# Front chunks of a hybrid trunk step: state inputs in two row groups copied out by ScalarE, scores and state outputs inside the first projection

## The reference

```python
proj = x @ w_in                                   # q, k, v (8 heads x 128) and u (1024)
attn = stick_breaking(q, k_all, v_all, q_pos, k_pos)
# per head: z = q k^T * scale; w = sigmoid(z) * prod of sigmoid(-z) of the later keys; out = w v
bu = einsum('blgc,gpc->blgp', u, b_bar)           # 64 groups x 64 complex states, 16 channels each
h = associative_scan(_linear_combine, (a, bu))    # h_t = lam_bar * h_(t-1) + bu_t
y = einsum('blgp,gcp->blgc', h, c).real + d_skip * u
z = gelu(y);  ssm = z * sigmoid(z @ w_glu + b_glu)
merged = [rms_norm(attn), rms_norm(ssm)]
```

## Time and profile before

| | us |
|---|---|
| median of 3 runs | 1701.26 |
| lowest, highest | 1698.42, 1701.41 |
| the profiled execution | 1701.27 |
| its span in the trace | 1699.5 |
| front: projection 0 of chunk 1 starts | 72.42 |
| front: last loop chunk ends | 383.58 |
| PE busy in the span | 1513.2 |

### The profile page before, as it was taken

How to read it: one execution, slowest core, us unless ns; L and a number is a source line. 1 busy time by engine, 2 the same in 40 slices (tenths; PEclk the granted TensorE clock), 3 DMA queues, 4 the chain that set the end, 5 groups by cost and what they waited for, 6 DMA issues and landing times.

```text
span 1699.5 us, 22977 instructions
## 1 busy us (share of the span) xinstructions
PE 1513.2 (89%) x8898; PEld 975.0 (57%) x8898; DVE 572.1 (34%) x1024; ACT 141.1 (8%) x296; POOL 225.8 (13%) x368
## 2 busy tenths in 40 slices
PE   8999999999999779999789898788898887889775
PEld 6777777777777546655445465454455454555333
DVE  7899988874210531111111021011112110111115
ACT  3111111113000300000000000000000000000001
POOL 4666666600000010000000000000000000000002
PEclk8999999999999889999999999999999999999997
DMA  7554544533496199999999999999999999999974
GB/s 182 152 139 110 147 120 118 139 98 102 143 303 221 40 346 412 404 416 415 416 400 416 418 404 410 415 414 405 399 417 411 389 417 413 412 407 412 417 271 171
DMA packets 175314, 520.04 MB, mean 306 GB/s; under 512 B 23504, under 2 KB 135248, under 8 KB 147952
## 3 DMA queue, kind: packets, MB, share of 16 engines
q1 hardware_dynamic: 160032, 485.73, 74.4%
q10 hardware_dynamic: 13056, 17.77, 3.3%
q0 software_dynamic: 2128, 15.21, 3.2%
HBM read 496.72 MB, written 21.95 MB: 305 GB/s over the span
## 4 chain that ended last, share of the span: by engine, by line
DMA 42%; PE 42%; DVE 9%; issue 4%; SPq 2%; POOL 1%; ACT 1%; ACTq 0%; DVEq 0%; POOLq 0%
DMA e_ring<-in_w_exp_up_dram 36%; PE bank L1016 12%; PE bank L1393 11%; PE bank L1412 4%; PE bank L1327 4%; DMA e_ring<-in_w_exp_gate_dram 4%; PE bank L1246 2%; PE bank L1176 2%; DVE e_ring L1580 2%; SPq L589 1%; PE bank L1068 1%; PE bank L1060 1%; DVE e_ring L1584 1%; DVE e_ring L1573 1%; DVE e_ring L1625 1%
## 5 line engine op out<-in xcount | busy, mean ns | idle before, releaser
L1393 PE MATMUL bank<-e_ring,xT_exp 128*64 128x256 f32 x4096 | 482.0, 394 | 94.0 <-DMA e_ring<-in_w_exp_gate_dram 60.4
L1393 PEld LDWEIGHTS bank<-e_ring,xT_exp 128*64 128x64 f32 x4096 | 298.5, 142 | 288.0 <-DMA e_ring<-in_w_exp_gate_dram 80.9
L1412 PE MATMUL bank<-e_ring,hidT 128*64 128x512 f32 x1024 | 243.2, 630 | 39.0 <-DVE hidT L1907 39.0
L1016 PE MATMUL bank<-xT,w_ring 128*128 128x288 f32 x1024 | 257.9, 410 | 0.7 <-issue 0.7
L1016 PEld LDWEIGHTS bank<-xT,w_ring 128*128 128x128 f32 x1024 | 193.0, 191 | 56.9 <-issue 5.1
L1902 DVE TENSOR_TENSOR hid<-bank,sig_exp 128x256 f32<-128x256 f32 x32 | 13.6, 425 | 557.3 <-ACT sig_exp L966 557.3
L1412 PEld LDWEIGHTS bank<-e_ring,hidT 128*64 128x64 f32 x1024 | 74.3, 144 | 186.0 <-issue 138.8
L762 POOL DMA_INDIRECT e_ring<-expert_rows_out,idx x6 | 5.6, 926 | 1058.4 <-ACT all_stored_mark L772 1056.9
L1327 PE MATMUL bank<-hT,w_ring 128*128 128x288 f32 (+2 forms) x640 | 137.2, 374 | 0.0
L1327 PEld LDWEIGHTS bank<-hT,w_ring 128*128 128x128 f32 x640 | 111.8, 193 | 20.1 <-issue 0.8
L1913 DVE COPY rows<-bank 128x512 f32<-128x512 f32 x32 | 22.1, 692 | 237.6 <-PE bank L1412 237.6
(11 more groups left out here) (317 smaller groups left out, 1223.3 us busy)
## 6 DMA issues: line engine op xcount, KB each, us to landing
e_ring<-in_w_exp_gate_dram SPq DMA_DIRECT2D x64, 2048.0 KB, 27.3
e_ring<-in_w_exp_up_dram SPq DMA_DIRECT2D x64, 2048.0 KB, 28.1
e_ring<-in_w_exp_down_dram SPq DMA_DIRECT2D x64, 2048.0 KB, 22.2
w_ring<-in_w_in_dram SPq DMA_DIRECT2D x32, 1024.0 KB, 6.2
w_ring<-in_w_out_dram SPq DMA_DIRECT2D x16, 1024.0 KB, 5.9
w_ring<-in_w_ple_gate_dram SPq DMA_DIRECT2D x16, 1024.0 KB, 23.9
expert_rows_out<-hT POOLq DMA_DIRECT2D x3, 1536.0 KB, 9.6
w_ring<-in_ssm_w_glu_dram SPq DMA_DIRECT2D x4, 1024.0 KB, 5.2
```

Source lines behind the costliest of these rows:

```text
L1016: last_mm = pe.matmul(out, weights(k), moving[:, k, :], start=(k == 0), stop=(k == n - 1))
L1393: mm = pe.matmul(gu[h * B:(h + 1) * B, s % 2, :], xT_exp[:, c, s // 2, :], w[:, c, h * FH:(h + 1) * FH], start=(s == 0 and c == 0), stop=( ...
L1412: mm = pe.matmul(bank[h * B:(h + 1) * B, 3 + n, :], hidT[:, c, half, :], e_ring[:, 2 * (NGU + half) + c, h * DH2 + n * 512:h * DH2 + (n + ...
```

## The change

Four things change in the front. The state inputs of two tiles are now made together: `bu(c, p, r)` makes part r (real or imaginary) of tiles 2p and 2p+1, two matmuls in two different row groups into banks 2 and 3, and ACT copies both banks into `bu_rows` in SBUF (`bu_copy`, 576 values); DVE's L1640 and L1641 read `bu_rows` in place of PSUM. The `bu` of tiles 0 and 1 stand inside projection 1 (at k = 3 and k = 6), those of tiles 2 and 3 between projections 2 and 3. The scores stand inside projection 0 at k = 4, and all four tiles' state outputs (`y_out`, now four column groups at once) at k = 11. On DVE the key scan and the weights come ahead of `du` and tile 0, and on ACT the sigmoids come ahead of the copy of u.

```diff
@@ ScalarE
+            def bu_copy(c, p, r):
+                act.wait_ge(bu_ready, c * 4 + 2 * p + r + 1)
+                act.wait_ge(bu_used, c * JC + 2 * p)
+                copy(bu_rows[:, r], bank[:, 2:4, 0:T]).then_inc(bu_copied, 1)
...
+            def chunk(c, prev, first):
+                if prev:
+                    weight_parts(c, first)
+                act.wait_ge(dense_done, c * 4 + 1)
...
+                copy(uT, bank[:, 0, 0:T]).then_inc(proj_copied, 1)
...
+                if prev:
+                    gelu_part(c, first)
+                bu_copy(c, 0, 0)
+                if prev:
+                    k_copy(c, first)
+                bu_copy(c, 0, 1)
...
@@ TensorE
-            def bu(c, i, first):
-                if not (first and i == 0):
-                    pe.wait_ge(bu_used, c * JC + i)
+            def bu(c, p, r, first):
...
+                    pe.wait_ge(bu_copied, c * 4 + 2 * p + r)
+                    pe.wait_ge(bcT_copied, c + 1)
+                    pe.wait_ge(proj_copied, c * 4 + 1)
+                for q in range(2):
+                    i = 2 * p + q
+                    mm = pe.matmul(bank[:, 2 + q, 0:T], bcT[32 * i:32 * i + 32, r, :], uT[32 * i:32 * i + 32, :], start=True, stop=True)
+                mm.then_inc(bu_ready, 1)
+
+            def y_out(c, first):
+
+                pe.wait_ge(h_ready, c * JC + JC)
+                if not first:
+                    pe.wait_ge(y_read, c)
                 for r in range(2):
-                    mm = pe.matmul(bank[:, 2 + r, 0:T], bcT[32 * i:32 * i + 32, r, :], uT[32 * i:32 * i + 32, :], start=True, stop=True)
-                mm.then_inc(bu_ready, 1)
...
+                    for i in range(JC):
...
+            def chunk(c, prev, first):
+
+                proj(c, 0, not prev, {4: (lambda: scores(c, first),), 11: (lambda: y_out(c - 1, first),)} if prev else {})
...
+                proj(c, 1, not prev, {3: (lambda: bu(c, 0, 0, not prev),) + ((lambda: k_turn(c),) if prev else ()),
+                                      6: (lambda: bu(c, 0, 1, False),)})
...
+                proj(c, 2, not prev)
+                bu(c, 1, 0, False)
                 if prev:
...
+                    v_turn(c, True)
+                    weights_turn(c)
+                bu(c, 1, 1, False)
+                proj(c, 3, not prev)
...
+            def last_chunk(c):
+
+                scores(c, False)
+                glu_start(0)
+                y_out(c - 1, False)
+                glu_start(1)
...
@@ VectorE
-                dve.wait_ge(bu_ready, n + 1)
-                own(dve.tensor_tensor(tmp1, bank[:, 2:4, 0:T], wre, ALU.mult))
-                dve.tensor_tensor(tmp2, bank[:, 2:4, 0:T], wim, ALU.mult).then_inc(bu_used, 1)
+                dve.wait_ge(bu_copied, c * 4 + 2 * (i // 2) + 2)
+                own(dve.tensor_tensor(tmp1, bu_rows[:, :, i % 2, :], wre, ALU.mult))
+                dve.tensor_tensor(tmp2, bu_rows[:, :, i % 2, :], wim, ALU.mult).then_inc(bu_used, 1)
...
-                    dve.wait_ge(y_part, c * 2 - 1 + i // 2)
+                    dve.wait_ge(y_part, c)
```

More of the change, by code:

```diff
@@ L354, in build @@
         bu_ready = sem("bu_ready")
+        bu_copied = sem("bu_copied")
         bu_used = sem("bu_used")
@@ new lines, in gelu_part, with k_copy @@
+            def gelu_part(c, first):
+                act.wait_ge(gelu_in, c)
+                if not first:
+                    act.wait_ge(z_done, c - 1)
+                act.activation(ysig, y2, ACT.Sigmoid, scale=2.0 * math.sqrt(2.0 / math.pi) * 0.044715).then_inc(gelu_sig, 1)
+            def k_copy(c, first):
+                act.wait_ge(kn_ready, c)
+                if not first:
+                    act.wait_ge(k_stored, (c - 1) * 32)
+                copy(k_nat[:, 0:2, :], bank[:, 7, 0:2 * P].rearrange("p (t n) -> p t n", t=2)).then_inc(kn_copied, 1)
+                copy(k_nat[0:TS, 2, :], bank[0:TS, 7, 2 * P:3 * P]).then_inc(kn_copied, 1)
@@ L876, in _ @@
-            chunk(LAST_C, False, True, False)
+                chunk(c, True, False)
+            last_chunk(LAST_C)
             act.wait_ge(a_copied, NCH)
@@ L1013, in _, with dense @@
         def _(pe):
-            def dense(out, weights, moving, n):
+            def dense(out, weights, moving, n, between={}):
                 for k in range(n):
+                    for step in between.get(k, ()):
+                        step()
                     last_mm = pe.matmul(out, weights(k), moving[:, k, :], start=(k == 0), stop=(k == n - 1))
@@ L1046, in _, with proj @@
             pe.wait_ge(par_copied, 1)
-            def proj(c, s, first):
+            def proj(c, s, first, between={}):
                 pe.wait_ge(w_landed[s], c * 16 + 16)
@@ L1164, in _, with scores @@
-            chunk(0, True, False, True)
-            chunk(1, True, True, True)
+            def scores(c, first):
+                pe.wait_ge(proj_copied, c * 4 - 1)
+                if not first:
+                    pe.wait_ge(wT_copied, (c - 1) * 2)
+                    pe.wait_ge(a_copied, c - 1)
+                pe.wait_ge(ckT_copied, c)
+                pe.matmul(bank[:, 5, 0:Z1], qT[:, 0:P], kT[:, 0:P], start=True, stop=True)
+                pe.matmul(bank[:, 5, Z1:Z2], qT[:, P:TP], kT[:, 0:TP], start=True, stop=True)
+                pe.matmul(bank[0:TS, 6, 0:PAST], qT[:, TP:T], ckT, start=True, stop=True)
+                pe.matmul(bank[0:TS, 6, PAST:PAST + TS], qT[:, TP:T], kT[:, TP:T], start=True, stop=True).then_inc(z_ready, 1)
@@ L1631, in chunk @@
                             v.then_inc(wgt_ready, 1)
+                if cur:
+                    own.wait()
+                    dve.wait_ge(proj_copied, c * 4 + 1)
+                    dve.tensor_scalar(du, uT, d_c, None, ALU.mult).then_inc(du_ready, 1)
+                    if prev:
+                        dve.wait_ge(table_ready, c)
+                    tile(c, 0, not prev)
+                if prev:
                     dve.wait_ge(gelu_sig, c)
```

292 lines of the change are left out of this document (131 added, 161 removed).

## The result

| | before | after |
|---|---|---|
| median of 4 runs each, us | 1701.34 | 1721.71 |
| lowest to highest | 1698.42 to 1706.39 | 1717.62 to 1723.26 |
| the profiled execution; its span | 1701.27; 1699.5 | 1720.82; 1719.1 |

A forecast was written before the change was run, and what follows sets the result against it. The prediction took one chain over PE and DVE, with POOL slowing DVE, to bound each turn. Six turns at +3.0 us and edges of +3, -1.65 and -1 gave +18.3, so 1719.5 us, range 1703 to 1729.

The forecast's parts named there:

- PE's work: PE per chunk: `bu` saves 2.0 us and `y_out` 1.1, so 43.73 falls to about 40.6 us.
- The new chain: From E over PE's queue (`y_out`, projections, transposes, `bu`) and ACT's copy to tile 0: 9.6 us, before 6.41.
- E: The end of a chunk's fourth tile on DVE, that is of its last product of h.
- The stand and the clock: PE stands 5.3 us a turn at k = 11; the clock falls to 0.50, costing 1.7 us (bounds 0 and 3.4).
- Tile 0 to E: DVE's tiles of a chunk, stretched by POOL's table: 36.35 us, where 33.7 was tiles before.
- the 2.1: Added us POOL costs DVE's tiles a turn: tile 1's first products read SBUF twice; scan and weights leave the stretch.
- The turn: One loop chunk: 45.95 us without the clock's cost, 47.65 with it, 3.0 longer than 44.64.
- The edges: Outside the middle turns: chunk 0 +3 us, last turn -1.65, last piece -1.
- The sum: Whole kernel: 3 + 6 x 3.0 - 1.65 - 1 = +18.3 us.
- faster outright: Rival, 0.10: DVE always full, turn 41.6 us, total 1683.7; gain once path plus POOL's cost is under 17.8 us.
- The clock holds: Rival, chance 0.13: the granted clock stays up through PE's stands, total 1707.6 us.
- POOL no dearer and the clock holds: Rival, chance 0.08: POOL costs DVE no more than before and the clock holds; turn 43.85 us, total 1695.

The follow-up runs named there:

- e1: Changed kernel with nine filler products on PE ahead of the wait for h at k = 11: 1717.32 us.
- e6: Changed kernel without the doubling steps of POOL's tables for chunks 2 to 7, output stale: 1676.90 us.
- e8: Changed kernel with both products of a `bu` pair in one row group, output not the reference's: 1730.81 us.
- e2: Changed kernel with `y_out` behind k = 15 of projection 0 and not at k = 11: 1707.22 us.
- e4: Kernel before the change, with only the scores moved to k = 4 of projection 0: 1704.78 us.
- e7: Kernel before the change, without the doubling steps of POOL's tables for chunks 2 to 7, output stale: 1696.25 us.
- e9: Kernel of e5 with `y_out` and C transposes at k = 8 of projection 1, a chunk's last `bu` at k = 5 of projection 3: 1690.53 us.
- e3: Changed kernel with `y_out` and C transposes moved to k = 13 of projection 1, off the way to tile 0: 1787.26 us.
- e5: Kernel of e3 with ACT's sigmoids behind the copies of uT and B and the two row copies: 1709.09 us.

## Why the prediction was right, point by point

- **PE's work.** A pair was to take 0.66 us and takes 0.69; `y_out` of four tiles was to take 1.1 and takes 1.11 at full clock (e1). PE's own work in a turn was to be 40.6; it is 40.46 (e6). e8 shows that the row group is the reason; the Trainium skill's rule for products in different row groups ("TensorE: Matmul & The Clock Gate", Part 3) agrees with it.
- **The new chain.** It is the forecast one: PE standing at k = 11, DVE waiting for the rows. From E to tile 0 I had 9.6 us without the clock. e1 measures 9.94: the hand-overs take 0.36 and not 0.15, and the pieces on PE 0.16 more than I had. e2, which takes only the ten records out, shows that this queue is the cause.
- **The stand and the clock.** 5.3 us forecast, 5.43 measured. The cost of 1.7 us came out as 1.74 (e1), though its working was off: I took half of a low stretch of 3.41 us, and the stretch lasts 6.83, of which 3.16 fall in the stand itself. The two errors cancel, so that the size came out is luck; that the clock falls, and on which instructions, is not. It costs six times and not seven, because PE is not early in the first turn.
- **Tile 0 to E.** 36.35 forecast, 36.02 measured. Without the table it is 28.13 (e6, 253.89 to 282.02), of which 1.69 is a wait ahead of tile 2 for its row copy. That leaves 26.44 for the tiles, where I had 26.85, and 36.02 - 26.44 = 9.6 for POOL, where I had 7.2 + 2.1 + 0.2 = 9.5. The size is right; the reason for its added part is so in small part only. I put it on the first two products of tile 1, which now read SBUF twice: they take 0.88 and 0.87, 0.1 more each. It is tile 2's second product that is long, 1.82 us at 306.16, and POOL's step beside it 1.73; in e4, where DVE still reads PSUM there, it takes 0.74 and POOL's same step 1.27 (timelines of DVE and POOL in e4, and of POOL in the changed kernel):

```profile
290.99 0.74 DVE L1578 TENSOR_TENSOR e_ring<-bank,rows 128x576 f32<-128x576 f32 x1
291.76 1.51 DVE L1580 TENSOR_TENSOR e_ring<-e_ring 128x288 f32<-128x288 f32 x1
```

```profile
290.46 1.27 POOL L508 TENSOR_TENSOR rows<-hT 128x512 f32<-128x512 f32 x1
```

```profile
305.63 1.73 POOL L510 TENSOR_TENSOR rows<-hT 128x512 f32<-128x512 f32 x1
```

The two run side by side in e4, and POOL's next step hits the sum behind (1.51, as 1.41 in the changed kernel), so this product is 1.1 us longer for its SBUF operand. But in e4 another place pays more (tile 1's four scans take 3.13 us, 2.67 in the changed kernel). DVE's busy time in a turn gives the whole: the table adds 9.1 us to it before (40.01 against 30.92 in e7) and 9.2 in the changed kernel (40.31 against 31.08 in e6). So hardly any of the 2.1 is new work for DVE. Most of it is hits that the scan, the weights and gelu's product bore before (4.63 us together, 3.06 in e7) and that now fall on the tiles. I had named both causes, but put the whole size on the first. By the rule of the Trainium skill ("SBUF — State Buffer", the section on the two separate sides) such instructions shut one another out whole; the trace agrees as to these times, since POOL's step ends at 307.36 and tile 2's product, begun at 306.16, ends 0.62 us later.
- **The turn.** 47.65 forecast, 47.48 to 47.73 in five turns; against before's 44.44 to 45.25 these are +2.4 to +3.1, and +1.3 in the first.
- **The edges** were the weak terms. Chunk 0's E came 5.1 us later (79.40 to 84.49), where I had +3. Half of that is not the change: in this execution the first transposes of chunk 0 already begin at 43.86 and not at 41.24, before anything that the change touches in the front, and in e1, whose chunk 0 is the same, they begin at 38.34 and E is at 79.79. From the first transposes to E it is 38.16 us before, 40.63 in the changed kernel and 41.45 in e1, so the +3 itself is borne out. The last turn was to be 1.65 shorter and is 0.09 longer (39.89 against 39.80): without the table there is the wait of 1.68 us ahead of tile 2, which I had left out. The last piece, from the last E to the transposes behind the last attention (414.03 before, 433.91 after), gave back 1.2, where I had 1. The turns were to add 18.0 and added 15.9. The sum was 18.3 and came out as 19.6 in the span. That it is so near is in part luck: the six turns are 2.1 under, the last one 1.7 over, and 2.6 are the later start of this one execution.
- **The kernel before.** I read its turn as one chain over both engines. e4 and e7 show less: PE's own work and its 0.91 us bound it, and DVE's 3.00 us for the scores were slack. The sum doesn't rest on this, but the gain that "faster outright" hoped for from these 3.00 us does.
- **The rivals.** "The clock holds" is what e1 made by force, and it gave 46.27 a turn, where I had 45.95. "POOL no dearer and the clock holds" and "faster outright" lacked their condition; but e6 and e9 show that both roads existed: the rival put the point of decision at 17.8 us for path and POOL's cost together; in e9 they are 43.25 - 26.85 = 16.4, and the kernel is faster.

Open: how much of e9's gain each of its parts (row groups, row copies, early scores, four tiles' `y_out`) brings. e4 shows that the scores alone bring nothing; the others, and the row copies above all, were not tried singly on the kernel before. The table's steps were only left out, not moved to another engine or time.

## What to carry to other kernels

When two engines hand work to one another once a turn and each waits for the other, as here for 5.4 and 5.1 us, the turn is the length of the path over both hand-overs, not the busy time of either. (With the table left out, the same queues were bound by PE's busy time, 40.46 us.) Work taken off the fuller engine is worth nothing if the wait is put in front of what the other engine needs next. Put a wait for the late engine behind everything that doesn't need it (here: the B transposes and the state inputs of the next chunk), and then read the other queues for a wait of the old order ahead of a copy that the new order needs early (e3 against e5: 78 us, the clock's part in it included). An engine that lengthens the bound one's instructions belongs into the sum: here the same change is worth -19 us without POOL's table and +20 with it.

## What was not expected of the hardware

Stands of 5.4 to 5.7 us brought low stretches of 6.83 us, one of 4.94 a stretch of 3.41, and stands of 2.9 to 3.4 us in e2 stretches of 3.41 or 6.83; stands of 1.4 us (e1) brought none. In e9 the clock fell at both stands of 2.2 us and not at those of 0.7 to 1.6. Filling a stand with products that nobody needs kept the clock at 1.00 and shortened a turn by 1.4 us; where PE is not early, the same filler costs its whole length. The part behind the front (from the first expert's second product to the end) took 1070.0 us in the changed kernel's execution and 1073.7 in e1's, with the same instructions; so differences of 3 us between single executions say nothing about the front.
